# Two plain pairs instead of one ahead of the seven-product loop of both SwiGLU FFNs, with the Pool's and the first down block's order changed

## The reference, cut to what matters

```
D_FF = 2816
h = rms_norm(x, norm_ffn[i])
x = x + swiglu(h, ffn_w_gate[i], ffn_w_up[i], ffn_w_down[i])   # silu(h @ gate) * (h @ up) @ down
```

## Time and profile before

| | us |
|---|---|
| median of 3 runs (lowest to highest) | 1549.85 (1549.19 to 1553.01) |
| the profiled execution, its span | 1549.58, 1547.8 |
| PE, DVE, ACT, POOL busy | 1484.3, 1064.2, 808.4, 443.4 |
| FFN 0 quartered loop | from about 73 to 284 |
| FFN 1 quartered loop | from about 623 to 832 |

### The profile page before, as it was taken

The page is one execution under the profiler, slowest core; times in us unless marked ns, Lnnn a source line. Parts: engine busy times, 40 slices in busy tenths (PEclk is TensorE's granted clock), DMA queues, the critical chain, the costliest instruction groups (busy, mean ns, idle before and its releaser), DMA issues.

```text
span 1547.8 us, 24388 instructions
## 1 busy us (share of the span) xinstructions
PE 1484.3 (96%) x8880; PEld 1292.4 (84%) x8880; DVE 1064.2 (69%) x1312; ACT 808.4 (52%) x1262; POOL 443.4 (29%) x273
## 2 busy tenths in 40 slices
PE   8889999999899999899999999999988999999997
PEld 8889999888797788899998887788667878888875
DVE  6599999542566425999997236335584689898885
ACT  5455555422455524555554224433683377787774
POOL 0577777200000004777773000000031012222211
PEclk9899999999999999999999999999999999999998
DMA  6023322323221031122333232222014379999994
GB/s 246 28 81 108 108 102 93 132 88 117 82 92 45 1 123 55 70 95 106 108 107 118 102 115 90 99 92 99 28 55 193 137 287 387 384 391 394 391 380 118
DMA packets 36215, 226.26 MB, mean 146 GB/s; under 512 B 5272, under 2 KB 5528, under 8 KB 11825
## 3 DMA queue, kind: packets, MB, share of 16 engines
q1 hardware_dynamic: 31392, 212.06, 35.8%
q0 software_dynamic: 4608, 13.22, 3.7%
q10 hardware_dynamic: 144, 0.03, 0.0%
HBM read 215.22 MB, written 13.63 MB: 148 GB/s over the span
## 4 chain that ended last, share of the span: by engine, by line
PE 52%; DVE 6%; DMA 3%; ACT 2%; issue 2%; DVEq 0%; ACTq 0%; POOLq 0%; SPq 0%
PE PS L268 16%; PE PS L270 15%; PE PS L269 15%; DMA eraw<-experts 3%; PE PS L1986 1%; DVE WL L263 1%; PE PS L2702 1%; DVE da_flat L2070 1%; PE PS L1997 1%; PE PS L2006 1%; DVE WEL L2836 1%; DVE da_flat L2084 0%; PE PS L1791 0%; PE PS L2352 0%; PE PS L2725 0%
## 5 line engine op out<-in xcount | busy, mean ns | idle before, releaser
L263 DVE TENSOR_TENSOR WL<-raw,WH 128x2048 fp32r<-128x2048 f32 x51 | 120.5, 2364 | 215.5 <-ACT WH L258 215.2
L2836 DVE TENSOR_TENSOR WEL<-eraw,WEH 128x2048 fp32r<-128x2048 f32 x96 | 217.5, 2287 | 20.6 <-ACT WEH L2773 20.5
L258 ACT ACTIVATE WH<-raw 128x2048 fp32r<-128x2048 f32 x49 | 93.8, 1914 | 222.1 <-PE PS L270 222.1
L2773 ACT ACTIVATE WEH<-eraw 128x2048 fp32r<-128x2048 f32 x96 | 182.3, 1914 | 33.8 <-DMA eraw<-experts 23.1
L891 DVE TENSOR_TENSOR WL<-plain,WH 128x512 fp32r<-128x512 f32 x152 | 171.2, 1126 | 24.0 <-ACT WH L785 21.8
L268 PE MATMUL PS<-AH,WL 128*128 128x256 f32 x608 | 176.0, 289 | 6.0 <-DVE AL L322 4.1
L270 PE MATMUL PS<-AH,WH 128*128 128x256 f32 x608 | 173.8, 286 | 0.0
L269 PE MATMUL PS<-AL,WH 128*128 128x256 f32 x608 | 173.6, 285 | 0.0
L268 PE MATMUL PS<-WH,AL 128*128 128x512 f32 (+2 forms) x416 | 155.8, 374 | 9.0 <-DVE WL L263 7.7
L891 DVE TENSOR_TENSOR WL<-raw,WH 128x512 fp32r<-128x512 f32 x120 | 161.3, 1344 | 0.9 <-ACT WH L785 0.9
L270 PE MATMUL PS<-WH,AH 128*128 128x512 f32 (+2 forms) x416 | 153.4, 369 | 0.0
(11 more groups left out here) (379 smaller groups left out, 3858.9 us busy)
## 6 DMA issues: line engine op xcount, KB each, us to landing
eraw<-experts SPq DMA_DIRECT2D x96, 1024.0 KB, 15.8
raw<-stream SPq DMA_DIRECT2D x94, 1024.0 KB, 4.8
out<-X SPq DMA_DIRECT2D x5, 512.0 KB, 2.7
moe_rows<-moe_rows_g SPq DMA_DIRECT2D x5, 512.0 KB, 3.8
X<-x SPq DMA_DIRECT2D x4, 512.0 KB, 5.6
ffn_row<-rows SPq DMA_DIRECT2D x2, 512.0 KB, 10.4
final_row<-rows SPq DMA_DIRECT2D x2, 512.0 KB, 6.2
cst<-consts SPq DMA_DIRECT2D x1, 739.5 KB, 13.5
```

What stands on the lines that cost most here:

```text
L258: act.activation(WH[:, u % SLOTS, :], raw[:, u % SLOTS, :], ACT.Copy).then_inc(unit_hi, 1)
L263: dve.tensor_tensor(WL[:, u % SLOTS, :], raw[:, u % SLOTS, :], WH[:, u % SLOTS, :].bitcast(F32), ALU.subtract).then_inc(unit_lo, 1)
L2773: act.activation(WEH[:, k % ESLOTS, :], eraw[:, k % ERAW, :], ACT.Copy).then_inc(unit_hi, 1)
L2836: dve.tensor_tensor(WEL[:, k % ESLOTS, :], eraw[:, k % ERAW, :], WEH[:, k % ESLOTS, :].bitcast(F32), ALU.subtract).then_inc(unit_lo, 1)
```

## The change

`PLAIN = 2`: the second pair is plain too, with all 512 tokens at once, and nine pairs are quartered. Its gate products go to banks 4 and 5, its up products to banks 2 and 3; ACT and DVE split its two units whole. POOL waits for the split of the last tile before its first rejoin. The token sums have a buffer of their own, `TF`, in the memory of `TL`: DVE writes the low part over the sum, and so waits until POOL has read it (sums 0 and 1). The first down unit is split in two halves, and PE begins with its first half for all four tiles.

```diff
-QUARTERED = FC - 2
+PLAIN = 2
+QUARTERED = FC - 2 * PLAIN
...
-            def unit_into(d, t):
+            def unit_into(d, t, halves=(0, 1)):
                 u = u0 + d
-                for f in range(2):
+                for f in halves:
                     for half in range(2):
                         w = slice(f * D + half * 512, f * D + half * 512 + 512)
                         j = 2 * DOWN_ORDER[d] + f
@@ -577,14 +578,21 @@
                                      d == 0 and f == 0, d == n - 1 and f == 1)
                 return mm
 
-            for d in range(n - 2):
+            ready(0, 0)
+            for t in ORDER:
+                first(t)
+                unit_into(0, t, (0,))
+            pe.wait_ge(unit_lo, u0 + 1)
+            ready(0)
+            for t in ORDER:
+                mm = unit_into(0, t, (1,))
+            mm.then_inc(unit_used, 1 + QUARTERED)
+            for d in range(1, n - 2):
...
+                with ExitStack() as soon:
+                    TF = sb(tag + "TF", [P, 4, 4, 256], F32, soon)
...
-                return HF[:, 6 + 2 * k:8 + 2 * k, :].rearrange("p a (b s) -> p (a b) s", s=256)
+                return TF[:, k, :, :]
...
-                    load_unit(sp, u0 + 2 + k)
-                with nc.sync.Fori(1, n) as i:
+                for k in range(2, 2 * PLAIN + 2):
+                    load_unit(sp, u0 + k)
+                with nc.sync.Fori(1, n - PLAIN + 1) as i:
                     for k in range(2):
...
+                for part, made in ((0, gate_made), (1, up_made)):
+                    pe.wait_ge(unit_lo, u0 + part + 3)
+                    if part:
+                        pe.wait_ge(c_made, 4)
+                    for k in range(2):
+                        pair(part, k, slice(0, S), (2 if part else 4) + k).then_inc(unit_used if k else made, 1)
+                pe.wait_ge(silu_made, 4)
+                with nc.Fori(PLAIN, n, engines=(mybir.EngineType.PE,), hint_back_edge=True) as i:
                     for odd in range(2):
...
-                def first_silu(k):
+                def plain_silu(i, k):
                     if k:
-                        act.wait_ge(unit_used, u0 + 1)
+                        act.wait_ge(unit_used, u0 + 2 * i + 1)
                     else:
-                        act.wait_ge(gate_made, 1)
-                    act.activation(silu[:, k, :], PS[:, k, :], ACT.Silu).then_inc(silu_made, 1)
+                        act.wait_ge(gate_made, i + 1)
+                    if i:
+                        act.wait_ge(c_made, 3 + k)
+                    act.activation(silu[:, k, :], PS[:, 4 * i + k, :], ACT.Silu).then_inc(silu_made, 1)
+
+                def down_hi(half):
+                    u = u0 + 2 * n
+                    w = slice(half * D, half * D + D)
+                    act.wait_ge(unit_landed[u % SLOTS], 16 * (u // SLOTS + 1))
+                    return act.activation(WH[:, u % SLOTS, w], raw[:, u % SLOTS, w], ACT.Copy)
...
                         h_high(2 * n - 4)
+                        down_hi(0).then_inc(q_hi, 1)
                         h_high(2 * n - 3)
...
                     else:
-                        u = u0 + 2 * n
-                        act.wait_ge(unit_landed[u % SLOTS], 16 * (u // SLOTS + 1))
-                        act.activation(WH[:, u % SLOTS, :], raw[:, u % SLOTS, :], ACT.Copy).then_inc(unit_hi,
-                                                                                                  1 + QUARTERED)
+                        down_hi(1).then_inc(unit_hi, 1 + QUARTERED)
...
-                first_silu(0)
+                plain_silu(0, 0)
+                plain_silu(0, 1)
+                split_hi(act, u0 + 2)
+                split_hi(act, u0 + 3)
                 sum_hi(0)
-                first_silu(1)
-                quarter_hi(0, 0, 0)
-                quarter_hi(1, 0, 0)
-                quarter_hi(2, 0, 0)
+                plain_silu(1, 0)
                 sum_hi(1)
-                quarter_hi(3, 0, 0)
-                act.wait_ge(unit_used, u0 + 2)
-                quarter_hi(4, 0, 0)
-                quarter_hi(5, 0, 0)
+                plain_silu(1, 1)
+                for q in range(4):
+                    quarter_hi(q, 0, 0)
                 sum_hi(2)
                 sum_hi(3)
-                quarter_hi(6, 0, 0)
-                with nc.scalar.Fori(1, n - 1) as i:
-                    unit(2 * i - 2, 0, 2 * i - 1)
-                    unit(2 * i - 1, 1, 2 * i)
+                act.wait_ge(unit_used, u0 + 4)
+                for q in range(4, 7):
+                    quarter_hi(q, 0, 0)
+                with nc.scalar.Fori(PLAIN, n - 1) as i:
...
+                    if k < 2:
+                        dve.wait_ge(rejoined, T + k + 2)
...
-                def first_h(k):
-                    dve.wait_ge(silu_made, k + 1)
+                def plain_h(i, k):
+                    dve.wait_ge(silu_made, 2 * i + k + 1)
                     if k:
-                        dve.wait_ge(unit_used, u0 + 2)
+                        dve.wait_ge(unit_used, u0 + 2 * i + 2)
                     else:
-                        dve.wait_ge(up_made, 1)
-                    dve.tensor_tensor(HF[:, k, :], silu[:, k, :], PS[:, 2 + k, :], ALU.mult).then_inc(c_made, 2)
+                        dve.wait_ge(up_made, i + 1)
+                    dve.tensor_tensor(HF[:, 2 * i + k, :], silu[:, k, :], PS[:, 2 + k, :], ALU.mult).then_inc(c_made, 1 + i)
...
                         h_low(2 * n - 4, 1)
+                        dve.wait_ge(q_hi, 7 * QUARTERED + 1)
+                        down_lo(0).then_inc(q_lo, 1)
                         h_low(2 * n - 3, 2)
...
-                    else:
-                        u = u0 + 2 * n
-                        dve.wait_ge(unit_hi, u + 1)
-                        dve.tensor_tensor(WL[:, u % SLOTS, :], raw[:, u % SLOTS, :], WH[:, u % SLOTS, :].bitcast(F32),
-                                          ALU.subtract).then_inc(unit_lo, 1 + QUARTERED)
...
+                    else:
+                        dve.wait_ge(unit_hi, u0 + 2 * n + 1)
+                        down_lo(1).then_inc(unit_lo, 1 + QUARTERED)
+
+                split_lo(dve, u0 + 2)
+                plain_h(0, 0)
+                plain_h(0, 1)
+                split_lo(dve, u0 + 3)
                 sum_lo(0)
-                quarter_lo(0, 0, 0)
-                quarter_lo(1, 0, 0)
-                first_h(0)
-                quarter_lo(2, 0, 0)
                 sum_lo(1)
-                quarter_lo(3, 0, 0)
-                first_h(1)
-                quarter_lo(4, 0, 0)
-                quarter_lo(5, 0, 0)
+                for q in range(4):
+                    quarter_lo(q, 0, 0)
                 sum_lo(2)
+                plain_h(1, 0)
                 sum_lo(3)
-                quarter_lo(6, 0, 0)
-                with nc.vector.Fori(1, n - 1) as i:
-                    unit(2 * i - 2, i, 0, 2 * i - 1)
-                    unit(2 * i - 1, i, 1, 2 * i)
+                plain_h(1, 1)
+                for q in range(4, 7):
+                    quarter_lo(q, 0, 0)
+                with nc.vector.Fori(PLAIN, n - 1) as i:
...
                 def rejoin_tile(t):
-                    pool.wait_ge(entered.lo, t + 1)
...
+                pool.wait_ge(entered.lo, T)
                 for t in range(T):
                     rejoin_tile(t)
```

More of the change, by code:

```diff
@@ L583, in down_by_tiles @@
                 for t in ORDER:
-                    if d == 0:
-                        first(t)
                     mm = unit_into(d, t)
-                mm.then_inc(unit_used, 1 if d else 1 + QUARTERED)
+                mm.then_inc(unit_used, 1)
             a, b = n - 2, n - 1
@@ L612, in hidden_memory @@
             FL = sb(tag + "FL", [P, FC, S], F32R, where)
-            return TH, TL, part, FH, HF, FL
+            return TH, TF, TL, part, FH, HF, FL
         def swiglu(block, tag, u0, silu, memory, entered, meanwhile, leave):
-            TH, TL, part, FH, HF, FL = memory
+            TH, TF, TL, part, FH, HF, FL = memory
             n = FC // 2
@@ L654, in sum_at @@
                 if isinstance(s, int) and s == 0:
-                    return HF[:, 2 + k, :].rearrange("p (c n) -> p c n", c=4)
+                    return HF[:, 6 + k, :].rearrange("p (c n) -> p c n", c=4)
                 return plain[:, k // 2, 0:4, 256 + P * (k % 2):256 + P * (k % 2) + P]
@@ L710, in _, with pair @@
             def _(pe):
-                def pair(part, k, tokens):
+                def pair(part, k, tokens, to):
                     slot = (u0 + part) % SLOTS
@@ L714, in pair @@
                         w = slice(c * 256 + k * P, c * 256 + k * P + P)
-                        mm = product(pe, PS[:, 2 * part + k, tokens], WH[:, slot, w], WL[:, slot, w],
+                        mm = product(pe, PS[:, to, tokens], WH[:, slot, w], WL[:, slot, w],
                                      AH[:, c, tokens], AL[:, c, tokens], c == 0, c == C - 1)
@@ L724, in _ @@
```

(15 more changed lines are left out.)

44 lines of the change are left out of this document (27 added, 17 removed).

## The result

| | kernel before | changed kernel |
|---|---|---|
| median of 4 runs (range), us | 1551.43 (1549.19 to 1554.54) | 1532.55 (1531.29 to 1533.31) |
| profiled execution, its span, us | 1549.58, 1547.8 | 1532.01, 1530.2 |

The ratio is 0.9876, 95% interval 0.9855 to 0.9897. The profiled time fell by 17.6 us; 15.9 were predicted. (The medians lie 18.9 us apart, because the kernel before has a fourth run here, 1554.54, that raised its median by 1.6.)

What follows compares the result with a forecast made beforehand. PE, busy 96%, was taken to bound the kernel, with stalls from POOL's chain. Gains 13.8 + 3.75 + 2.49 less 4.16 made 15.9 us, so 1549.6 - 15.9 = 1533.7, said as 1534; range 1529.5 to 1541.

Steps and rivals of the forecast that it cites:

- The bound: Whole kernel: PE busy 96%; time to be had from its idle stretches, lower clock and matmul columns; POOL's chain causes the stall.
- Old stalls: First quartered unit of both FFNs: idle and slow stretches go, 8.06 us in FFN 0 and 5.75 in FFN 1, together 13.8.
- Price of the plain pair: Second pair: plain 22.20 us against quartered 20.12, a cost of 2.08 us an FFN, 4.2 for both.
- (a): Second pair's start: DVE's split of unit u0+2 comes in time, 0.15 us to spare in FFN 0, 0.6 in FFN 1.
- (b): Third pair's weights and POOL's sums behind them: quarter splits ready by 93 and 95, PE there at 95.5; nothing waits.
- (c): ACT's `copy_out` in the first quartered unit: done by 97.6, asked for at 99.8, two microseconds to spare.
- Entries: Both FFN entries: POOL's later start shortens DVE's instructions there, gaining 2.12 us in FFN 0 and 1.63 in FFN 1.
- The clock at FFN 0's entry: Slow stretch at FFN 0's entry: may shorten by up to 2.70 us or lengthen by as much; taken as 0.
- Down halves: First down unit in both FFNs: PE's waits for DVE's whole split go, gain 2.49 us, bounds 0 and 2.49.
- the term of 1.27: FFN 0's first down unit: PE's wait of 1.27 us for DVE's split goes.

Runs made afterwards that it cites:

- e3: Kernel before with one edit: POOL waits for the last tile's split before its first rejoin, second pair still quartered; 1560.39 us, ratio 1.0063.
- e4: Changed kernel with POOL waiting per tile and the first down unit split whole again, so the plain second pair alone; 1538.63 us, ratio 0.9919.
- e1: Changed kernel with POOL's rejoins waiting tile by tile again, as before the change; 1537.82 us, ratio 0.9912.
- e7: Changed kernel with POOL's first rejoin released by the third tile's split in place of the fourth; 1534.20 us, ratio 0.9888.
- e9: Changed kernel with the first down unit split whole again and no hint on the back edge of PE's loop; 1538.34 us, ratio 0.9925.
- e6: Changed kernel with PE's loop over the quartered pairs kept, but without the hint on its back edge; 1532.71 us, ratio 0.9884.
- e5: Changed kernel with PE's loop over the nine quartered pairs written out as straight code in both FFNs; 1533.19 us, ratio 0.9892.
- e8: Changed kernel with POOL's first rejoin released by the third tile's split and no hint on PE's loop; 1530.23 us, ratio 0.9864.

## Why the prediction was right, and its steps

**The bound, right.** PE's stalls were the time to be had, and POOL's chain was behind them (e3).

**Old stalls, right.** No bracket of them is left, and the granted clock does not fall behind FFN 0's entry until 404 us, nor in FFN 1's pairs. The cause was read rightly too: the stall's end moved with POOL's first token sum (e3), and the plain pair alone shortened the bodies by 11.2 us (e4).

**Price of the plain pair, mis-sized.** It measured 21.79 us, not 22.2, and a quartered pair 20.26, not 20.12 (turn to turn in the loop), so it cost 1.53 and not 2.08. I had taken the spacing of 512-column matmuls from FFN 0's down products, as 0.2312 us; in the plain pair they start 0.227 us apart. That is twice 0.55 us of the surplus gain.

**(a) The split of u0+2, right.** In FFN 0 it was ready 0.19 us before it was needed. The turns of DVE and POOL held: DVE ended 2.16 us after POOL's rejoin, although another POOL instruction was ready. The page "SBUF — State Buffer" of the Trainium skill, section "Who interferes with whom", has it that the later one waits for the whole of the other's instruction, and for one instruction the trace agrees; for a queue of them the trace adds the turn. DVE had also asked first each time (here at 66.70, POOL's next at 67.55), so the traces show no more than that the one who asked first came next.

**(b) and (c), the first quartered unit, right; the second not looked at.** I followed POOL's chain to the first unit of the loop and stopped. One pair later ACT waited for a POOL sum until 115.91, and PE stood still for 0.82 us. e1 and e7 show this wait, with the smaller ones beside it, to be the price of the late POOL, 1.2 us in all.

**Entries, right.** 2.11 and 1.74 against 2.12 and 1.63; e1 takes both back. The clock at FFN 0's entry, put at 0 with bounds of 2.70 either way, gave 0.64: the first matmul of 256 columns still takes 0.58 us, as in the earlier trace rows, but 18 matmuls ran at the lower clock and not 25.

**Down halves, half right.** 1.2 us in FFN 1. In FFN 0 the term of 1.27 failed: PE's gap at the loop's end replaced the wait for the split and was 0.5 us longer. With the gap gone the halves bring their 1.1 (e9 against e6). In the trace of before PE stood still for 1.27 us in all at this place, so at most that much of such a gap can have been hidden behind the wait for the split; whether there was any is not shown. Whoever sees PE wait for one thing knows only that every other wait there ends no later.

**The stalls, sized from their brackets.** A bracket counts from the modelled end of the last matmul, 0.28 us behind its start, while the next would have started 0.12 us behind it. So each wait costs PE 0.16 us more than its bracket says: in FFN 1 the start-to-start steps of 2.39, 2.44 and 1.50 us cost 2.27, 2.32 and 1.38, for brackets of 2.11, 2.16 and 1.22. With 0.11 for the slow first matmul at 630.12 that is 0.6 us in FFN 1 that the prediction left out; for the one stall in FFN 0 it is 0.15.

**The sum.** Predicted 15.9, measured 17.6. In favour went 1.1 from the price of the two plain pairs, 0.7 from the stalls as just told, 0.1 at FFN 1's entry, 0.6 at the start (ahead of all edits), 0.6 from the clock behind FFN 0's entry and 0.7 behind FFN 1's first down product. Against it went 0.6 for small waits in FFN 0 (1.2 in the changed kernel, 0.6 of the same kind before, counted by steps) and 1.8 for the down term of FFN 0. That makes 15.9 + 3.8 - 2.4 = 17.3. So the mechanism was right, but that the median came within 1.5 us of the forecast is in part luck: errors of 3.8 and 2.4 us stood against each other, and 1.9 of the 3.8 (start, clock, end) lie in stretches that differ by as much between kernels with the same code there.

## What to carry to other kernels

A stall whose bracket names a copy on ACT can be made by the engine that ACT's queue waits for: follow the queue back, and delay that engine alone to prove it. Price a stall from start to start, not by its bracket. Cover moved in front of a preamble is worth more than its price when it hides several engines' chains, but follow each chain one turn further than the place where it used to stall. Where a gap's releaser ended a microsecond earlier, or reads `issue`, suspect the engine's own loop, and try the loop with and without its hint.

## What the runs showed of the hardware

- The end of a PE loop with a hint on the back edge left a gap of 1.48 to 1.99 us in FFN 0 in the seven traces of kernels with the hint and a plain second pair, and none of its own in FFN 1. With no hint or with the loop written out there was none (e5, e6, e8; in e9 PE waits 1.27 us for DVE there). In the kernel before and e3, also with the hint, PE stood still for 1.27 us in all.
- DVE and POOL instructions that read SBUF twice took turns when both engines had some queued; in the cases read, the one that had asked first came next. DVE's split took 2.93 us against 2.29, POOL's token sum 4.35 against 2.41 (e7).
- At a granted clock of 1.00, 128x512 matmuls start 0.227 us apart in the plain pair and in FFN 1's down products, and 0.233 apart in FFN 0's, in every trace. The two FFNs' down products have the same shapes and order; why they differ is open.
- From FFN 1's first down product to the end, where e5, e7 and the changed kernel have the same code, the traces take from 711.8 us (e5) to 716.1 (e7), and three traces of the same changed kernel 713.6, 714.5 and 715.2. The granted clock near 1220 us is 0.50 from 1216 to 1232 in e7 and from 1214 to 1222 in e8. A gain of 1 or 2 us is read from rows, or from several gains added up as in e8, not from one median.
